# Splitting two key projections on TensorE: one around decay products, one in quarters between small products

## What is computed

```python
h = rms_norm(x, norm_mix[l])
proj = h @ w_in[l]                                  # 256 x 1024 times 1024 x IN_COLS
u_pool, u_rwkv, u_nsa = split_cols(proj, [...])
# RWKV: decay and rate come from two small "LoRA" products, inner size 32
u = u + (u_prev - u) * mu                           # r, k, v, wd, ad, gd
w_log = -softplus(-(w0 + tanh(wd) @ w_up)) - 0.5    # "decay products": wup
a = sigmoid(a0 + ad @ a_up)                         # "rate products": aup
bonus = sum(r_h * k_h * r_k, axis=-1) * v_h         # "bonus sums": a product with ones per head
# sparse attention, keys of the compressed branch
kc_blk = gelu(blocks @ w1) @ w2                     # "compressed keys" kcb (and values vcb)
lc = einsum(q, kc_blk) + bias                       # "compressed scores" cs, softmax over 15 blocks
ls = einsum(q, k_sel) + bias_s                      # uses the selected keys k_s: projection "ks"
```

## Time and profile before

| | us |
|---|---|
| median of three runs | 665.17 |
| the profiled execution, on the device | 663.23 |
| its span, first to last instruction | 661.4 |
| TensorE busy in the span | 609.6 |
| weight loads of TensorE busy (beside it) | 444.7 |
| VectorE busy | 215.7 |
| ScalarE busy | 141.0 |

### The profile page before, as it was taken

The page is one execution under the profiler, slowest core; times in us unless marked ns, Lnnn a source line. Parts: engine busy times, 40 slices in busy tenths (PEclk is TensorE's granted clock), DMA queues, the critical chain, the costliest instruction groups (busy, mean ns, idle before and its releaser), DMA issues.

```text
span 661.4 us, 11707 instructions
## 1 busy us (share of the span) xinstructions
PE 609.6 (92%) x4934; PEld 444.7 (67%) x4934; DVE 215.7 (33%) x592; ACT 141.0 (21%) x354; POOL 20.1 (3%) x23
## 2 busy tenths in 40 slices
PE   5999999999999999999999999998989888948674
PEld 5888887888887777877778888886344433414231
DVE  3152448524332665346520222226111212012022
ACT  2010243131234263343431000001200111010013
POOL 1000000001100003000000000000000000000000
PEclk9999999999999999999999999999999999969798
DMA  8385334731301111101137995797999999999993
GB/s 353 133 333 182 117 142 172 273 128 64 108 23 65 66 64 65 34 34 66 64 128 286 420 422 207 274 425 264 401 421 420 422 420 421 420 421 422 419 393 117
DMA packets 27143, 158.94 MB, mean 240 GB/s; under 512 B 2880, under 2 KB 7120, under 8 KB 9168
## 3 DMA queue, kind: packets, MB, share of 16 engines
q1 hardware_dynamic: 24080, 137.71, 53.2%
q10 hardware_dynamic: 3008, 20.45, 7.4%
HBM read 157.07 MB, written 1.07 MB: 239 GB/s over the span
## 4 chain that ended last, share of the span: by engine, by line
PE 66%; issue 31%; ACT 1%; DMA 1%; DVE 0%; POOL 0%; SPq 0%; POOLq 0%; ACTq 0%; DVEq 0%
PE bank L606 47%; PE bank L804 5%; PE bank L902 2%; PE bank L931 2%; PE bank L951 2%; PE bank L961 1%; PE bank L915 1%; PE bank L1021 1%; PE bank L836 1%; DMA table<-params 1%; PE bank L627 1%; PE bank L866 1%; PE bank L971 1%; PE bank L855 1%; PE bank L1099 0%
## 5 line engine op out<-in xcount | busy, mean ns | idle before, releaser
L606 PE MATMUL bank<-hT,ring 128*128 128x256 f32 (+2 forms) x960 | 215.0, 377 | 0.0
L606 PEld LDWEIGHTS bank<-hT,ring 128*128 128x128 f32 (+2 forms) x960 | 173.6, 190 | 31.9 <-issue 11.9
L606 PE MATMUL bank<-yT,ring 128*128 128x256 f32 x256 | 55.4, 379 | 0.0
L606 PEld LDWEIGHTS bank<-yT,ring 128*128 128x128 f32 x256 | 48.6, 190 | 6.6
L1382 ACT ACTIVATE work<-bank 128x512 f32<-128x512 f32 (+1 forms) x42 | 21.5, 511 | 114.7 <-PE bank L1203 48.9
L1249 PE MATMUL bank<-ring,work 128*32 128x512 f32 (+1 forms) x192 | 35.2, 659 | 10.3 <-DMA yT<-experts 7.2
L1741 DVE TENSOR_TENSOR work<-bank,table 128x512 f32<-128x512 f32 (+1 forms) x22 | 11.6, 544 | 97.4 <-PE bank L1196 89.6
L1196 PEld LDWEIGHTS bank<-work,tok 128*128 128x128 f32 x256 | 30.2, 192 | 10.0 <-issue 10.0
L1196 PE MATMUL bank<-work,tok 128*128 128x128 f32 x256 | 31.5, 278 | 0.8 <-DVE work L1745 0.8
L1542 ACT ACTIVATE tok<-tok,small 128x128 f32<-128x128 f32 (+1 forms) x64 | 28.5, 445 | 14.5 <-DVE small L1959 12.6
L1257 PE MATMUL bank<-work 128*128 128x512 f32 (+1 forms) x68 | 29.9, 581 | 0.5 <-DVE work L2306 0.5
(11 more groups left out here) (249 smaller groups left out, 705.1 us busy)
## 6 DMA issues: line engine op xcount, KB each, us to landing
ring<-front SPq DMA_DIRECT2D x48, 1024.0 KB, 4.8
ring<-experts SPq DMA_DIRECT2D x40, 1024.0 KB, 25.3
work<-experts SPq DMA_DIRECT2D x9, 1024.0 KB, 27.0
ring<-experts ACTq DMA_DIRECT2D x8, 1024.0 KB, 14.0
table<-experts SPq DMA_DIRECT2D x6, 1024.0 KB, 27.1
yT<-experts SPq DMA_DIRECT2D x6, 1024.0 KB, 26.5
hT<-experts SPq DMA_DIRECT2D x4, 1024.0 KB, 24.6
work<-experts ACTq DMA_DIRECT2D x3, 1024.0 KB, 28.0
```

The source lines that it names most:

```text
L606: return first(pe.matmul(o, l, r, start=(k == 0), stop=(k == n - 1)))
```

## The change

`project` gets an inner part, `project_part`, that does one half, or a range of k of one half. With it two projections are cut up. No instruction is added or dropped, and no stream but TensorE's is touched: ScalarE, VectorE and SyncE keep their orders, and the bank plan stays.

```diff
+            def project_part(o, n, m, ks=range(KD)):
+                w = chunk(n).rearrange("p (k c) -> p k c", k=KD)
+                for k in ks:
+                    last = mm(o[:, m * S:(m + 1) * S], w[:, k, m * P:(m + 1) * P], hT[:, k, :], k, KD)
+                return last
...
-            for c in range(1, 7):
+            for c in range(1, 6):
                 project(f"rkv{c}", C_K + c - 1)
+            rkv6 = begin("rkv6")
+            project_part(rkv6, C_K + 5, 0)
             pe.wait_ge(q["lora_w_ready"], 1)
             ... wup0, wup1 ...
+            end(project_part(rkv6, C_K + 5, 1), "rkv6")
+            pe_take()
             ... aup0, aup1 (their matmuls now pass through first()) ...
...
             ... hidT ...
-            project("ks", C_KS)
+            ks = begin("ks")
+            project_part(ks, C_KS, 0)
             pe.wait_ge(q["hidT_ready"], 1)
             ... kcb, vcb ...
-            pe.wait_ge(q["bonus_ready"], 1)
-            for n in range(2):
-                o = begin(f"bonus{n}")
-                end(pe.matmul(o[:, :], cn("headsum"), mix[...], start=True, stop=True), f"bonus{n}")
+            project_part(ks, C_KS, 1, range(KD // 2))
...
             pe.wait_ge(q["q_ready"], 4)
             pe.wait_ge(q["cmp_kv_ready"], 2)
-            for i in range(NT):
+            def compressed(i):
                 ... one cs{i} ...
+            compressed(0)
+            pe.wait_ge(q["bonus_ready"], 1)
+            for n in range(2):
+                ... bonus{n} ...
+            compressed(1)
+            end(project_part(ks, C_KS, 1, range(KD // 2, KD)), "ks")
+            pe_take()
             early(RWKV_STEPS[0])      # tok00, tok01
             late(RWKV_STEPS[0])       # tok02, atok0
```

More of the change, by code:

```diff
@@ L606, in mm @@
                 return first(pe.matmul(o, l, r, start=(k == 0), stop=(k == n - 1)))
+            def project_part(o, n, m, ks=range(KD)):
[3 more added lines that the diff above has]
+                return last
             def project(name, n):
-                w = chunk(n).rearrange("p (k c) -> p k c", k=KD)
                 o = begin(name)
                 for m in range(2):
-                    for k in range(KD):
-                        last = mm(o[:, m * S:(m + 1) * S], w[:, k, m * P:(m + 1) * P], hT[:, k, :], k, KD)
+                    last = project_part(o, n, m)
                 end(last, name)
@@ L668, in _ @@
                     c = (2 * n + m) * P
-                    last = pe.matmul(o[:, m * S:(m + 1) * S], pr("lora_up")[32:64, c:c + P], mix[32:64, 12, :],
-                                     start=True, stop=True)
+                    last = first(pe.matmul(o[:, m * S:(m + 1) * S], pr("lora_up")[32:64, c:c + P], mix[32:64, 12, :],
+                                           start=True, stop=True))
                 end(last, f"aup{n}")
@@ L724, in _ @@
             end(last, "vcb")
-            pe.wait_ge(q["bonus_ready"], 1)
-            for n in range(2):
-                o = begin(f"bonus{n}")
-                end(pe.matmul(o[:, :], cn("headsum"), mix[:, 4 + 2 * n:6 + 2 * n, :], start=True, stop=True), f"bonus{n}")
+            project_part(ks, C_KS, 1, range(KD // 2))
             def values(name, c, i):
@@ L973, in _ @@
                 end(last, f"cs{i}")
+            compressed(0)
+            pe.wait_ge(q["bonus_ready"], 1)
+            for n in range(2):
+                o = begin(f"bonus{n}")
+                end(pe.matmul(o[:, :], cn("headsum"), mix[:, 4 + 2 * n:6 + 2 * n, :], start=True, stop=True), f"bonus{n}")
+            compressed(1)
+            end(project_part(ks, C_KS, 1, range(KD // 2, KD)), "ks")
+            pe_take()
             early(RWKV_STEPS[0])
```

## The result

| | median, us | runs | against before |
|---|---|---|---|
| before | 665.07 | 22 | |
| after the change | 667.33 | 22 | ratio 1.0032, 95% interval 1.0021 to 1.0042: +2.1 us, 1.4 to 2.8 |

The change makes the kernel slower, by 0.32%. That is inside the range and on the side that was forecast, but the forecast's +3.2 us lies just outside the interval of what was measured, so about 1.1 us of the sum has to be found. The profiled execution of the changed kernel took 666.23 us on the device (span 664.4), 3.0 us more than that of before.

The account below looks back on a forecast made before the run. TensorE was taken to bound the kernel up to 445 us, the experts' weight transfers from 465 us, with TensorE's losses reaching the end. 1.14 + 0 + 2.07 = +3.2 us gave 668.4 us; 8-in-10 range 665.6 to 670.4.

Parts of the forecast that it names:

- the forecast's +3.2 us: Whole kernel: 1.14 + 0 + 2.07 us added, giving 668.4 us against the median.
- The first place: rkv6 cut around wup and aup: 0.95 us of lost overlap plus 0.19 us for shape changes, +1.14 us.
- The second place: ks in quarters: reordered work itself 0, but TensorE idle +2.07 us before atok0, waiting for ScalarE's ks and tok00 copies.
- the forecast's 148.47 on the old axis: Start of atok0, behind ScalarE's four ks copies and tok00, on the old time axis; before it started at 146.40.
- The rival of hidden weight loads: Compressed scores: several weight loads fetched ahead hide beside wide and bonus matmuls, -3.0 us, giving 665.4 us; chance 0.09.
- The forecast's first rival: At the end: expert transfers, not TensorE, set it, so part or all of 3.2 us vanishes, 665.2 us; chance 0.10.
- half a per cent: Whole kernel: about what a measurement can tell from no change, 3.3 us.
- The prediction's check on the transfers: Behind the mixers: experts' transfers saturate about 3.2 us later; wrong if line 915's shift isn't found again at 455 us.

Follow-up runs that it names:

- e3: Changed kernel with ScalarE's four copies of the ks keys moved behind those of the turned blocks; -0.3 us (-1.2 to +0.7) against before.
- e5: Kernel before with only ks in quarters, plus ScalarE's ks copies behind those of the turned blocks; -1.1 us (-2.2 to +0.1) against before.
- e9: Kernel before, unchanged, one more profiled execution; line 915 came 1.3 us after the 153.89 of the first profile.
- e10: Kernel before, unchanged, another profiled execution after e9; no time of its own given in the experiments.
- e1: Changed kernel with ks put back as before, leaving only rkv6 cut in halves around wup, aup behind it; +1.5 us (0.0 to 2.9) against before.
- e4: Kernel before with 32 identity products of 256 columns, 13.8 us of TensorE's time, in front of cs0; +11.2 us (9.8 to 12.6) against before.
- e8: Kernel before with 8 identity products of 256 columns, 3.5 us, in front of cs0; +1.9 us (0.7 to 3.0) against before.
- e11: Changed kernel, unchanged, one more profiled execution; no time of its own given in the experiments.
- e2: Kernel before with only ks cut in quarters, rkv6 and the decay products as before; +3.1 us (2.0 to 4.2) against before.
- e6: e5 with wup and aup matmuls issued in turns; -3.7 us (-5.1 to -2.3) against before, median 662.69.
- e12: e6 with each step's share of gate matmuls issued in one piece; -3.0 us (-4.2 to -1.7) against before, median 661.25.
- e7: Kernel before with the matmuls of cs0 and cs1 issued twice, 3.6 us of load-bound instructions; +5.3 us (3.4 to 7.2) against before.

## Why it came out so

**The first place, as forecast.** +1.14 us of lost overlap and shape changes. The sets take 1.92 us each, to the row. e3 and e5 differ by this place alone: `kw` starts 1.15 us later in the one and 0.05 earlier in the other.

**The second place, as forecast.** +2.07 us of wait: 13.78 us of work against 13.69, and 1.94 us idle before `atok0` (the forecast's 148.47 on the old axis is 149.58 less the first place's 1.1). e3 shows by one edit that it is ScalarE's order. The rival of hidden weight loads is out: `cs0` behind eight wide matmuls takes 140.85 - 139.15 = 1.70 us for 16. That is 0.11 us each for all but the first, as in the old order.

**The term that was missing** was put at nothing in half a sentence of the prediction: "at a granted clock of 1.00, which is 2.4 GHz, so there is no clock to win". The clock was read from one execution, and four of six profiled executions with this order lose clock at this place, though not that one. (The stretches named for it, do not even cover 131 to 175 us; there too it was 1.00.) The profiles, for 138 to 165 us:

| second place in | clock in each profile | us lost to it |
|---|---|---|
| before's order (before, e9, e10, e1, e4, e8) | 1.00, 0.94, 0.94, 0.87, 0.94, 1.00 | 0, 1.6, 1.6, 3.3, 1.6, 0: mean 1.3 |
| quarters (after, e11, e2, e3, e5, e6, e12) | 1.00, 1.00, 0.94, 1.00, 1.00, 1.00, 1.00 | 1.7 in e2: mean 0.2 |

e7, which doubles the load-bound run, is left out; it had 0.81 and lost 4.9 us.

The losses are worked out from the shift of TensorE's starts between the first compression matmul (117 us) and line 915, less what was added. In before's order the stretch from `kcb` to the turned blocks is 8.5 us of matmuls with 128 columns or fewer, with 1.8 us of wide bonus products in it. The quarters break it with wide ones, and of seven profiles only e2's, where the idle time follows, has a fall. So the missing term is about 0.2 - 1.3 = -1.1 us, and 1.14 + 2.07 - 1.1 = 2.1 us, which is what was measured. That it comes out to the tenth is luck: each mean is over six or seven profiles of different kernels, with losses from 0 to 3.3 us, and this sum was made after the result. Nor do the two places have to add up. In e2 the wait ends at 148.85, in the changed kernel at 149.58; the one profile of the first has a fall behind it and the two of the second have none. Whether that is a matter of when the wait comes was not tested.

By the Trainium skill ("TensorE: Matmul & The Clock Gate", Part 4: PE-mode transpose) transposes don't count as busy the way matmuls do. The traces don't decide whether that is at work here: the falls of e9 and e10 begin within the turned blocks, which are transposes, but that of e1 begins 1.4 us ahead of them and that of e7 6.7 us ahead, among the compressed scores.

**All executions, not only the profiled ones.** The record lists the mean granted clock of every execution from e1 on, and of the changed kernel's 22. The 67 executions of before that were timed beside e1 to e12 have clocks from 0.966 to 0.982, 0.9750 in the mean, and the lower the clock, the longer the time: 0.36 us for each 0.001, with a correlation of -0.82. The changed kernel's 22 have 0.9783 in the mean, and none is under 0.972 where 12 of the 67 are. 3.3 thousandths at 0.36 us are 1.2 us: the missing term again, by another way. And the executions at 0.978 or more are 664.0 us in the mean before (16) and 667.0 after (13), 2.9 us apart, close to the forecast's 3.2. Within one set it is the same: e3, e5 and e12, all with quarters, have 0.9767, 0.9772 and 0.9782 where the executions of before beside them have 0.9743, 0.9748 and 0.9763; e1, in before's order, has 0.9740 beside 0.9743. e2 has the quarters and the wait, and 0.9747 beside 0.9743: it gained no clock, which fits its +3.1. These means don't tell where in an execution the clock was lost, and the changed kernel's 22 were timed in another set than the 67, so they support the account and don't prove it.

**A second place where the clock falls** lies behind the mixers, where TensorE begins to wait for the experts' weights. From before and from e10, both the same kernel, and from e5:

```profile
445.00:480.00 35.00, 31.32 (x218) 17.60 (x217) 12.94 (x62) 6.94 (x19) 0.73 (x1) 1.00 0.86 338
445.00:480.00 35.00, 31.45 (x192) 18.84 (x191) 12.91 (x62) 5.75 (x17) 0.73 (x1) 0.90 0.81 321
445.00:480.00 35.00, 31.33 (x212) 17.92 (x214) 12.94 (x62) 6.35 (x18) 0.74 (x1) 0.95 0.82 320
```

If each instruction of TensorE is set beside the same one of the first profile of before, the shift at any point can be read (in us; for the end, the difference of the spans):

| | shift at 155 us | at 450 us | clock, 445 to 480 | at the end |
|---|---|---|---|---|
| e9 | 1.3 | 1.3 | 1.00 | 1.6 |
| e10 | 1.8 | 1.8 | 0.90 | 3.2 |
| e1 | 4.9 | 4.9 | 0.90 | 7.1 |
| e4 | 16.1 | 16.1 | 0.92 | 16.7 |
| e8 | 3.9 | 3.9 | 1.00 | 3.5 |
| e7 | 7.6 | 7.5 | 1.00 | 7.3 |
| after | 3.2 | 3.2 | 1.00 | 3.0 |
| e11 | 2.9 | 2.9 | 1.00 | 3.4 |
| e2 | 4.1 | 4.1 | 1.00 | 4.9 |
| e3 | 1.1 | 1.1 | 0.95 | 2.4 |
| e5 | -0.1 | -0.1 | 0.95 | 2.1 |
| e6 | -0.9 | -0.9 | 1.00 | -0.3 |

Two things follow. Between 155 and 450 us nothing is absorbed, in any profile. And the five executions with a fall between 445 and 480 us lose 1.5 us from 450 us to the end, in the mean, where the seven without lose 0.2. These falls come in both orders (e10, e1, e4; e3, e5), so by these counts they favour neither, but they are a good part of the spread of single executions, and part of why e1's profiled one was slow: 1.1 us of its 7.1 are work, 3.3 the first fall, 2.2 come behind 450 us. A profile's end is thus a poor check on a term of a microsecond; the shift at 450 us is a good one.

The same account for the rest, as work and waits added, plus the fall in the kernel's own profile, less 1.3 for before's mean. It sets the fall of one execution against the times of many, so it can only be rough:

| | added | fall seen | sum less 1.3 | measured |
|---|---|---|---|---|
| after | 3.2 | 0 | 1.9 | 2.1 (1.4 to 2.8) |
| e1 | 1.1 | 3.3 | 3.1 | 1.5 (0.0 to 2.9) |
| e2 | 2.1 | 1.7 | 2.5 | 3.1 (2.0 to 4.2) |
| e3 | 1.1 | 0 | -0.2 | -0.3 (-1.2 to 0.7) |
| e4 | 13.8 | 1.6 | 14.1 | 11.2 (9.8 to 12.6) |
| e5 | 0 | 0 | -1.3 | -1.1 (-2.2 to 0.1) |
| e6 | -0.7 | 0 | -2.0 | -3.7 (-5.1 to -2.3) |
| e7 | 3.5 | 4.9 | 7.1 | 5.3 (3.4 to 7.2) |
| e8 | 3.5 | 0 | 2.2 | 1.9 (0.7 to 3.0) |

Six of nine lie inside. e1 misses by 0.2, and its profile was its slowest run; with the mean fall of 1.3 it would be 1.1. The profile of e4, 679.91 us, was the slowest of its five too, with a clock of 0.973 where the other four have 0.976 to 0.981. Had those no fall at this place, the sum would be 13.8 - 1.3 = 12.5 us, just inside; their falls were not recorded, so this is an estimate.

**What stays open.** e4 is 2.9 us short of its account as it stands in the table, and e6 is 1.7 us ahead of its own. The forecast's first rival, that a part of a shift is lost before the end, would by the factor of 0.81 from e4 make the sum of 3.2 into 2.6, also inside the interval of the change. The profiles speak against it as far as 450 us: the 13.8 us of e4 are there in full, and its end is 16.7 us late. Behind 450 us they don't rule out a small loss, since shifts there change by -0.4 to +0.8 us even without a fall between 445 and 480 us. Against the factor alone also speak e3 and e5, which have nothing to scale down to -0.3 and -1.1. The account of the clock rests on 13 profiles and on the mean clock of all executions; that the fall is there is shown, that it is rarer with the quarters is well supported (one of seven profiles against four of six, and the mean clocks), its share to a tenth is not shown. Nor was the measurement as coarse as the prediction took it to be, half a per cent: with 22 executions of each the interval is 0.1% to either side.

The prediction's check on the transfers held: in the changed kernel's profile the DMA share falls between the same two long runs of transfers as in the earlier trace rows, about 3 us later, so that 445 to 450 us is now full:

```profile
445.00:450.00 5.00, 5.00 (x32) 4.54 (x32) 1.98 (x7) 0.00 (x0) 0.00 (x0) 1.00 1.01 421
450.00:455.00 5.00, 4.91 (x46) 4.80 (x45) 1.95 (x10) 0.99 (x3) 0.00 (x0) 1.00 0.46 187
```

## What to carry to other kernels

Before a product is moved later, follow its reader: an engine that takes its work in order will stand before it, and everything behind it in its stream waits too; here moving four copies back in ScalarE's order gave the 2 us back. Small matmuls on different rows of the array have to be issued in turns to run side by side; cutting them apart loses the overlap and pays for the change of shape. And a clock of 1.00 in one profile is one execution's: where a long stretch of load-bound matmuls stands on the path, take several profiles, and compare the mean clock of all executions, before writing that there is nothing to win.

## What the runs showed of the hardware

- Two sets of eight 32-row matmuls took 2.9 us one set after the other, 2.2 us in turns, and 3.8 us apart; a change between 32-row and full-array matmuls costs 0.19 us, in either direction.
- With TensorE shown 27.00 of 27.00 us busy, the clock still fell to 1.2 GHz in four of six executions, in a run of load-bound matmuls and transposes. To be shown busy did not keep the clock.
- The mean granted clock of an execution goes with its time: over 67 executions of one kernel 0.36 us for each 0.001.
- 3.5 us of load-bound matmuls more cost 5.3 us at the end, 3.5 us of wide ones in the same place 1.9 us.
